# A decoder step on one core: the split activations and feed-forward rows are stored four columns further along

## The reference

```python
def swiglu(h, wg, wu, wd):
    return (jax.nn.silu(h @ wg) * (h @ wu)) @ wd

def trunk(x, p, pos, h0_re, h0_im, build_kv, w):
    for i in range(DEPTH):
        hn = rmsnorm(x, w['norm_mix_g'][i])
        ...
        x = x + o
        x = x + swiglu(rmsnorm(x, w['norm_ffn_g'][i]), w['ffn_w_gate'][i],
                       w['ffn_w_up'][i], w['ffn_w_down'][i])
        gate = jax.nn.sigmoid(rmsnorm(x, w['norm_ple_g'][i]) @ w['ple_w_gate'][i])
        x = x + gate * (p[i] @ w['ple_w_proj'][i])
```

## Time and profile before

| what | value |
|---|---|
| median of 3 runs | 3291.53 us (3290.84 to 3291.8) |
| profiled execution, its own time | 3290.61 us |
| its span, first to last instruction | 3288.8 us |
| PE busy | 3204.2 us, 97% |
| PEld busy | 3053.8 us, 93% |
| DVE, ACT, POOL busy | 62%, 47%, 16% |
| granted TensorE clock, mean | 0.989 |
| HBM traffic | 189 GB/s over the span |

### The profile page before, as it was taken

The page is one execution under the profiler, slowest core; times in us unless marked ns, Lnnn a source line. Parts: engine busy times, 40 slices in busy tenths (PEclk is TensorE's granted clock), DMA queues, the critical chain, the costliest instruction groups (busy, mean ns, idle before and its releaser), DMA issues.

```text
span 3288.8 us, 69205 instructions
## 1 busy us (share of the span) xinstructions
PE 3204.2 (97%) x27708; PEld 3053.8 (93%) x27708; DVE 2032.7 (62%) x2281; ACT 1554.2 (47%) x1927; POOL 540.5 (16%) x477
## 2 busy tenths in 40 slices
PE   7999999999999999999999999998999999999998
PEld 6899888889999999999999997855999999999998
DVE  7999988865655544555665546454665554455566
ACT  4555555644544444444554433343554444444454
POOL 5666566620000000000000006000000000000000
PEclk9999999999999999999999999999999999999999
DMA  6444554456565555655556658888565655665553
GB/s 178 145 145 144 166 156 147 146 158 186 167 184 176 186 184 176 186 174 191 170 184 190 185 192 290 285 294 289 177 189 173 191 181 183 178 184 181 184 172 133
DMA packets 384392, 608.42 MB, mean 185 GB/s; under 512 B 52537, under 2 KB 144986, under 8 KB 383882
## 3 DMA queue, kind: packets, MB, share of 16 engines
q1 hardware_dynamic: 351738, 539.06, 53.0%
q10 hardware_dynamic: 29392, 60.86, 5.4%
q0 software_dynamic: 3024, 5.22, 0.4%
HBM read 594.83 MB, written 26.94 MB: 189 GB/s over the span
## 4 chain that ended last, share of the span: by engine, by line
PE 78%; DVE 13%; POOL 2%; issue 2%; ACT 2%; DMA 1%; SPq 0%; ACTq 0%; DVEq 0%; POOLq 0%
PE psum L407 22%; PE psum L408 22%; PE psum L409 22%; DVE rows_rest L1344 2%; PE psum L2338 2%; DVE turned L1403 2%; POOL prod_pool L1557 2%; PE psum L1023 1%; PE psum L2348 1%; PE psum L2386 1%; DVE normed_chunk L1428 1%; DVE turned L1394 1%; DVE state_ri L1411 1%; PE psum L1044 1%; PE psum L1045 1%
## 5 line engine op out<-in xcount | busy, mean ns | idle before, releaser
L390 DVE TENSOR_TENSOR w_rest<-w_raw,w_head 128x1024 fp32r<-128x1024 f32 x776 | 972.8, 1266 | 950.1 <-ACT w_head L386 949.3
L386 ACT ACTIVATE w_head<-w_raw 128x1024 fp32r<-128x1024 f32 x776 | 907.7, 1183 | 942.8 <-PE psum L409 907.4
L407 PE MATMUL psum<-act_head,w_head 128*128 128x264 f32 x4224 | 1202.5, 285 | 6.3 <-DVE act_rest L2788 5.2
L408 PE MATMUL psum<-act_rest,w_head 128*128 128x264 f32 x4224 | 1199.5, 284 | 0.0
L409 PE MATMUL psum<-act_head,w_rest 128*128 128x264 f32 x4224 | 1199.1, 284 | 0.0
L407 PEld LDWEIGHTS psum<-act_head,w_head 128*128 128x128 f32 x4224 | 822.6, 195 | 7.4 <-issue 5.6
L408 PEld LDWEIGHTS psum<-act_rest,w_head 128*128 128x128 f32 x4224 | 823.5, 195 | 0.2
L409 PEld LDWEIGHTS psum<-act_head,w_rest 128*128 128x128 f32 x4224 | 823.1, 195 | 0.0
L407 PE MATMUL psum<-hid_head,w_head 128*128 128x264 f32 x1408 | 399.5, 284 | 0.0
L408 PE MATMUL psum<-hid_rest,w_head 128*128 128x264 f32 x1408 | 399.3, 284 | 0.0
L409 PE MATMUL psum<-hid_head,w_rest 128*128 128x264 f32 x1408 | 399.2, 284 | 0.0
(11 more groups left out here) (421 smaller groups left out, 4083.9 us busy)
## 6 DMA issues: line engine op xcount, KB each, us to landing
w_raw<-in_ffn_w_gate SPq DMA_DIRECT2D x176, 512.0 KB, 4.3
w_raw<-in_ffn_w_up SPq DMA_DIRECT2D x176, 512.0 KB, 4.4
w_raw<-in_ffn_w_down SPq DMA_DIRECT2D x176, 512.0 KB, 3.7
w_raw<-in_cache_cmp_k SPq DMA_DIRECT2D x256, 128.0 KB, 2.6
w_raw<-in_cache_cmp_v SPq DMA_DIRECT2D x256, 128.0 KB, 2.6
w_raw<-in_ssm_w_glu SPq DMA_DIRECT2D x64, 512.0 KB, 3.9
w_raw<-in_ple_w_gate SPq DMA_DIRECT2D x64, 512.0 KB, 4.4
w_raw<-in_kv_w SPq DMA_DIRECT2D x48, 512.0 KB, 3.8
```

Source lines behind the costliest of these rows:

```text
L386: nc.scalar.activation(pairs(WH, u), tiles_of(RAW, u), ACT.Copy).then_inc(head_done, 1)
L390: nc.vector.tensor_tensor(pairs(WL, u), tiles_of(RAW, u), pairs(WH, u).bitcast(F32), ALU.subtract).then_inc(rest_done, 1)
L407: nc.tensor.matmul(o, wh, head, start=k == 0, stop=False)
L408: nc.tensor.matmul(o, wh, rest, start=False, stop=False)
```

## The change

`act_head` and `act_rest` become two views of one tensor, `act_split`, with four unused columns (16 bytes) in front and four behind; `hid_head` and `hid_rest` likewise of `hid_split`; `y_full` (`YF`), which shares the place of `act_head`, is moved with it. The chunks of `act_*` then begin 144 bytes over a multiple of 256 and go up by 32 (144, 176, 208, 240, 16, 48, 80, 112). As the tensor has grown by 32 bytes, all that is placed behind it lies 32 bytes further: the three weight rings at 160 modulo 256, `ple_head` at 160, `ple_rest` at 32, and `hid_split` at 32, so its chunks at 48, 80, 112, 144 and so on. `rows_rest0` and the tensors placed at `xh_at` and `xl_at` stay where they are, but for `taps_next`, 32 bytes further. On every engine the instructions, their shapes and their order are the same as before; addresses alone differ.

```diff
     X = sb("x_res", [P, KC, T])
+    LEFT = 4
+
+    def shifted(name, chunks, dtype, at=None):
+        whole = sb(name, [P, 2 * LEFT + chunks * T], dtype, at=at)
+        return whole[:, LEFT:LEFT + chunks * T].rearrange("p (k n) -> p k n", n=T)
+
     xh_at = sb.at
-    XH = sb("act_head", [P, KC, T], F32R)
-    xl_at = sb.at
-    XL = sb("act_rest", [P, KC, T], F32R)
+    acts = shifted("act_split", 2 * KC, F32R)
+    XH, XL = acts[:, 0:KC, :], acts[:, KC:2 * KC, :]
+    xl_at = xh_at + KC * T * 4
...
-    YF = sb("y_full", [P, KC, T], at=xh_at)
-    TAPS_NEXT = sb("taps_next", [P, 2, SLOT], at=xh_at + 8 * T * 4)
+    YF = shifted("y_full", KC, F32, at=xh_at)
+    TAPS_NEXT = sb("taps_next", [P, 2, SLOT], at=xh_at + 8 * T * 4 + 8 * LEFT)
...
-    HH = sb("hid_head", [P, FC1, T], F32R, at=region)
-    HL = sb("hid_rest", [P, FC1, T], F32R, at=region + FC1 * T * 4)
+    hids = shifted("hid_split", 2 * FC1, F32R, at=region)
+    HH, HL = hids[:, 0:FC1, :], hids[:, FC1:2 * FC1, :]
```

## The result

The changed kernel takes 3296.40 us (median of 20 runs, 3291.27 to 3299.75), the kernel before 3289.47 (20 runs beside them on the same chip, 3286.59 to 3292.3). The ratio is 1.0019, with a 95% interval of 1.0013 to 1.0025: slower by 6.9 us (4.3 to 8.2 by the interval), where 0.22% faster was forecast.

What follows compares the result with a forecast made beforehand. PE was taken to bound the kernel. 7.5 us from 188 slow chunks less 0.2, all else 0, took the span from 3288.8 to 3281.5; 1.8 around it and 0.9 to the median gave 3284.2 us, range 3282.5 to 3299.5.

Steps and rivals of the forecast that it cites:

- What bounds the kernel: Feed-forward stretch: PE is busy 700.00 of 700 us, other engines are ahead, so time off its matmuls comes off the end.
- The 7.3 us: Split-activation and hidden-row chunks: 188 slow ones falling to 1.44 us give 7.5 us, less 0.2 for 6 chunks.
- If the slow case is tied to that one place: Condition of the gain: only chunks beginning at 128 modulo 256 are slow, so all 188 fall to 1.44 us.
- I take nothing: Weight rings and all else behind the split activations lie 32 bytes further; this was taken to cost 0.
- a meeting: Possibility that moving stream and weight loading meet in memory, so the weights' shift to 160 counts; sum still 7.3 us.
- The 16 bytes at 0: Backward streams beginning on odd multiples of 16, a place not seen in the trace: cost taken as 0, at most 22 us.
- The bound of 22 us from the gates' pace: Upper limit for the odd 16 bytes: all 18,624 matmuls at the gates' 121.7 ns instead of 120.5 lose 22 us.
- Still one chunk in eight: Rival, chance 0.25: the slow place is 32 bytes wide, so 144 or 112 stays slow; time stays 3291.5 us.
- Two in eight: Rival, chance 0.08: chunks at 112 and 144 are both fully slow, 188 more at 0.04, plus 7.5 us, 3299.0.
- All streams lose their step: Rival, chance 0.12: 16 bytes between chunks' and weights' grids make every matmul jitter, from -2 to +22 us.
- Third to fifth part: DMA targets 32 bytes past multiples of 128, first-stage rows partly moved, ple's second halves staying 2.92 us: each taken at 0.

## Why the prediction was wrong, by its own steps

The forecast was 7.3 us less, and 6.9 more was measured. The 3296.4 us lie in the stated range only through the share of the rivals.

**What bounds the kernel** was right: a half of 23.19 us in place of 23.13 came out at the end, and no other engine moved.

**The 7.3 us** failed at "If the slow case is tied to that one place". With the chunks on multiples of 32, the slow place is that of the weights: 128 before, 160 with the weights 32 on, and with the weights at 0 or at 144 no chunk at 128 has more than some 8 ns over. That all 188 slow chunks lay at 128 was read from a kernel in which the weights lay at 128 too, so the rows could not tell the two apart, and the earlier trace rows already hinted at the second.

**"I take nothing"** for the weights' shift of 32 holds for the shift by itself: the kernel before with that shift alone kept its span of 3288.8 us. What failed is the answer on the two shifts together. The prediction did ask what a meeting would do, and answered that at odd multiples of 16 both keep clear. They don't: chunks at odd multiples of 16 pay 0.0665 us in eight against weights at 160 and 0.074 against weights at 176. The Trainium skill's rule in "TensorE: Matmul & The Clock Gate", Part 2, step 1, that loading the next weights takes no read bandwidth from the running matmul, doesn't make the weights' place indifferent here: moving the weights alone took a half from 23.13 to 23.05 us.

**The 16 bytes at 0** is the term that this comes down to. The sum took this cost at nothing because rows stream forwards from such places at 120.0 ns; it measured 5.4 us, 13.0 of extra instead of 7.6. The bound of 22 us from the gates' pace was far too high. Of the 14.2 us between the forecast difference and the measured one, 7.3 are the gain that didn't come and 5.4 this cost; the other 1.5 are within the interval.

**The rivals.** "Still one chunk in eight" was right in its pattern, with 144 slow in the trace. Its reason, a place that is slow by itself, is not: 128 was slow through the weights, and of 144 no run shows it. Its price was mis-sized: 0.04 us was taken for 144 as for 128, and it measured 0.0665, at eight places more. With both, and from the 3289.5 us of the 20 runs (the three of the prediction lay 2 us higher), it gives 3294.9, against 3296.4. "Two in eight" asked for 0.075 us of the two neighbours to be slower by 0.2%; 144 did nearly that alone (60 ns, and 6.5 in the chunk after it; 112 is plain), and with the eight more places the time came to the edge of it. "All streams lose their step" didn't happen: the others stay at 1.441.

**Third to fifth part** were right as far as a run can tell: glu's first matmul starts at 663.6 us where it started at 664.0, the stretch 1975 to 2300 has 0.88 and 291 GB/s where it had 0.87 and 290, and ple's half kept 2.92 us. Attention's length moved by 4 us between two executions of the same kernel, so a change of 1 us there would not be seen.

**What stays open.** Four corners are measured, as ns over eight plain chunks: chunks and weights on multiples of 32, 40.5; chunks off and weights on, 66.5; both off, 74; chunks on and weights off, 0 but for a few chunks with 8. Neither address nor distance alone gives this, since distances of -16 and +16 are free in the last and dear in the second. One rival stands untested for the changed kernel: chunks at 144 are slow with the weights at 160 and at 176, so 144 may be slow by itself among odd multiples of 16, with the weights setting the price (60 and 41 ns). Its weights moved by 32 alone would tell. Why the side on which the odd 16 lies decides isn't known from these runs, nor why 120 and 136 stand out with chunks on odd multiples of 8. That it is the memory's side on which the two reads meet is argued only.

## What to carry to other kernels

A regular extra on one chunk in eight is worth a list of all operands that the instruction and its neighbours read, with the address of each: here the weights' address was a constant modulo 256, and so couldn't be seen as a cause. Before shifting the many, shift the one: 16 bytes ahead of the weight rings gave 0.15% (0.06 to 0.24), while 16 bytes ahead of the activations took 0.19. And keep such moving operands on multiples of 16 bytes, since 8 off it cost 2.2 to 2.3% of this kernel.

## What the runs showed of the hardware

The address of the stationary operand modulo 256 changes the pace of the moving stream, by up to 60 ns in 12 matmuls of 264 columns (the changed kernel's chunk 0; 0 with the weights at 144 and chunks at multiples of 32). A moving operand at an odd multiple of 8 bytes costs 4.2 to 4.4 ns a matmul, 120.1 to 124.5. Head and rest of one chunk 64 bytes apart modulo 256 cost 13 to 27 ns in 12 matmuls. Attention varied between 354.1 and 358.3 us in executions of one kernel.
